# Halves at the sublayer ends, another order in the differential attention, and its causal mask added by TensorE

## The chip, the cores and the metric

One NeuronCore of a Trainium2 chip runs the whole program. The metric is the device time in microseconds; the kernel before takes 2036.5 us (median of 3 runs, 2032.58 to 2038.41).

## The reference

The model has two blocks over 256 tokens of width 1024, in float32. The first block is a four-branch mixer and a mixture of 16 experts. The second has six sublayers, each of the form `x + gate * rmsnorm(f(modulate(rmsnorm(x))))`: feed-forward, sparse attention, feed-forward, then feed-forward, differential attention, feed-forward. The differential attention, cut:

```python
q = apply_rope(proj[..., :B_QK].reshape(B, S, 2, B_HEADS, B_HEAD_DIM), cos, sin)
k = apply_rope(proj[..., B_QK:2 * B_QK].reshape(B, S, 2, B_HEADS, B_HEAD_DIM), cos, sin)
v = proj[..., 2 * B_QK:].reshape(B, S, B_HEADS, B_V_DIM)
s = jnp.einsum('btchd,bschd->bchts', q_b, k32) * scale      # per block of 128 queries
s = jnp.where(causal, s, -jnp.inf)
p = jax.nn.softmax(s, axis=-1)
a = p[:, 0] - lam_val * p[:, 1]
o = jnp.einsum('bhts,bshe->bthe', a, v32)
o = rmsnorm(o, subln_g) * (1.0 - lam_init)
```

## The kernel before

Every engine has its own program, written out by hand; they meet through semaphores. `see(name)` waits for one more count of a name, `mark`, `tell` and a name given to an operation add one. All helpers record one line (`mm` L803, `f` L1740, `stt` L2300, `tt` L2293), so an operation is told by its tiles. Tokens are in two tiles `i` of 128. Weights come in units of 1 MB by SP's queue into a ring of six slots. For products at float32 precision ScalarE rounds a unit (`w_hi`) and VectorE forms the rest (`w_lo`); three matmuls replace one.

**Sublayer ends.** `turnover` (ScalarE and VectorE) and `turn_normed` (TensorE) join two sublayers. For tile 0: when `out` is told, ScalarE takes the squares of the product, VectorE scales it (`out_rows`) and adds it to `xs` (`residual`), ScalarE squares `xs` (`row_squares`), VectorE writes the normed `h` (`pre_norm`, told as `turnable`), and TensorE turns `h` by matmuls with the identity on top of the shift (`turn_normed`, `preset_shift`), from where `columns` takes the operand of the next sublayer. Then tile 1. In a feed-forward, `four_tiles` does four tiles of 128 hidden columns: gate and up of one, down of the one before, for both token tiles; it runs in a loop of four rounds, and two further hidden tiles end the sublayer: down for tile 0, `out`, down for tile 1, `out`.

**Differential attention.** `differential` (TensorE), `a_differential` (ScalarE), `v_differential` (VectorE). Sixteen projection steps give queries and keys (columns 0 to 1023 and 1024 to 2047 of `proj`). VectorE ropes all of them after the last, TensorE turns them in groups of four through banks 2 and 3 and ScalarE copies them to `qT_d` and `kT_d` (`turned`). Eight units `n` follow: query tile `i = n // 4`, two heads of two components each, keys 128 for `i` 0 and 256 for `i` 1. The scores of all units use banks 0 and 1. The order is:

- TensorE, unit n: scores(n+2), values(n+1), a projection step of 24 matmuls whose result later products need, wait for `p_ready`, transposes of the probabilities, wait for ScalarE's copy (`pt_out`), P·V into banks 4 to 7.
- ScalarE, unit n: exponentials of unit n+1 (`softmax_exps`), copy of values(n+1), copy of the transposes, wait for P·V (`o_psum`), and for `i` 1 the square of it.
- VectorE, unit n: `masked_rows` of unit n+1 (scale and mask from PSUM to an SBUF buffer, told as `s_read`; maxima, told as `nmax`), then the reciprocals and the difference of unit n (`p_ready`).

scores(n) wait for `s_read` of unit n-1. Between rope and first unit VectorE also splits unit 11, forms lambda, and prepares the gains and the shift of this and the next sublayer (`out_gain`, `in_gain`, `split_shift`). The sparse sublayer has the same kind of loop, with two bank pairs (`score_bank`), a mask added by a matmul of the identity with `keep`, and exponentials out of PSUM.

Of the kernel before, what the change touches and what calls it, by code (L numbers as in the profile page):

```python
# [21 lines left out]
ALU = mybir.AluOpType  # L22
ACT = mybir.ActivationFunctionType
AX = mybir.AxisListType

S = 256
# [244 lines left out]
def build(nc, A, out):  # L271
# [54 lines left out]
    with ctx:  # L326
# [166 lines left out]
        qT_d, kT_d = by_slot[(first + 6) % R], by_slot[(first + 7) % R]  # L493
# [29 lines left out]
        bigs_d = big_d, acc[:, 0, :].rearrange("p (a b) -> p a b", b=S)  # L523
# [267 lines left out]
        def _(pe):  # L791
# [36 lines left out]
            def turn_normed(n, i):  # L828
# [8 lines left out]
                t.see("turnable")  # L837
                for b in range(2):
                    for k in range(4):
# [492 lines left out]
            def four_tiles(n0, r, h0):  # L1332

                wide = [None, None]
                for f in range(4):
# [10 lines left out]
                    x = down(g, 128, wd, g % 2, r * 4 + (h0 + g + 1), start=False, stop=False)  # L1346
# [164 lines left out]
            def ffn(n):  # L1511
# [6 lines left out]
                with pe.Fori(chunks % 4, 4) as r:  # L1518
                    four_tiles(n0 + 6, r, h0 + 4)
                    if chunks == 4:  # L1520
                        sum_chunk(r, c0)
                m, k0 = n0 + 30, h0 + 20
# [4 lines left out]
                for i in range(2):  # L1527
                    x = down(3, 128, held, 1, k0, False, False, (i,))
# [118 lines left out]
            def differential(sub):  # L1647
                n0 = unit[0]
                for n in range(16):
                    project_step(sub, DIFF_COLS, n)  # L1650
                unit[0] += len(DIFF_COLS)
                values_from = t.sent["proj"]

                def values(n):
# [4 lines left out]
                    t.tell(one_tile(P[:, 3 if n else 7, 0:256], i, w), "proj")  # L1659
# [3 lines left out]
                for i in range(2):  # L1663
                    turns([proj[:, i, 128 * k:128 * k + 128] for k in range(16)])
# [3 lines left out]
                def scores(n):  # L1668
                    i, hg = units[n]
                    kw = 128 * (i + 1)  # L1670
                    if n >= 1:
                        pe.wait_ge(sem("s_read"), n)
                    else:
                        pe.wait_ge(sem("proj_out"), values_from)
                    for k in range(4):
# [4 lines left out]
                               kT_d[r, tile, 0:kw])  # L1680
# [6 lines left out]
                scores(0)  # L1687
                scores(1)
                for n, (i, hg) in enumerate(units):
                    if n + 2 < len(units):  # L1690
                        scores(n + 2)
                    if n + 1 < len(units):
                        values(n + 1)
                    if n == 7:
                        pe.wait_ge(sem("s_read"), 8)
# [40 lines left out]
        def _(act):  # L1736
# [357 lines left out]

            def out_squares(n, i):
# [11 lines left out]
            def turnover(n, kind):  # L2107
# [6 lines left out]
                row_squares(0)  # L2114
# [109 lines left out]
            def values_out(n):  # L2224
# [3 lines left out]
                f(proj[:, i, 2048 + u * 256:2304 + u * 256], P[:, 3 if n else 7, 0:256], ACT.Copy, "proj_out")  # L2228
# [969 lines left out]
```

## Time and profile before

| | us |
|---|---|
| median of 3 runs | 2036.5 |
| profiled execution, device time | 2034.79 |
| its span | 2033.0 |
| busy: TensorE, VectorE, ScalarE, GpSimd | 1913.7, 1396.7, 974.6, 80.4 |
| mean granted TensorE clock | 0.973 |
| code loaded (queue 8) | 1.21 MB, 0.2% of the DMA engines' span |

Times below are microseconds from the first instruction of the span. A bracket behind a row is the engine's idle time before it and who ended that. The granted clock is a share of 2.4 GHz; 0.50 is 1.2 GHz. Matmuls overlap by a few hundredths, so their busy times add to slightly more than the time between starts.

### The profile page before, as it was taken

Reading aid. Unit: us, or ns where it says so; the run is one execution under the profiler, and the core shown is the slowest. Engines: PE = TensorE matmul, PEld = TensorE weight load, DVE = VectorE, ACT = ScalarE, POOL = GpSimd, SP = SyncE. Lnnn points to the kernel's source line nnn. Section 1 sums busy time; section 2 is a strip of 40 time slices with the busy share of each in tenths; the row PEclk is TensorE's granted clock in tenths of the full one; section 3 lists DMA queues with packets and bytes.
Section 4 is the critical chain, followed back from the end, with each engine's and each line's share of the span. In section 5 each row is a group of like instructions: output and inputs, shape, how many; then the busy total and the mean of one; then the engine's idle time right before and its main releaser. Section 6 shows DMA issues by size and latency. Waiting matters only on the chain.

```text
span 2033.0 us, 30145 instructions
## 1 busy us (share of the span) xinstructions
PE 1913.7 (94%) x12007; PEld 1646.7 (81%) x12007; DVE 1396.7 (69%) x1877; ACT 974.6 (48%) x1377; POOL 80.4 (4%) x173
## 2 busy tenths in 40 slices
PE   8999999989899999997999978999999999789998
PEld 7988687878588888876999864899989989648997
DVE  3873444536799889897788684588768875746754
ACT  4664402223577777764333545434444345564432
POOL 6000000000000000000000000000000000000000
PEclk9999999979899999998999989999999999899999
DMA  8443432126999999994897521599579957136652
GB/s 259 148 147 123 145 104 83 43 102 222 390 330 346 349 324 340 367 345 136 302 321 260 192 83 42 202 323 326 175 255 324 324 176 235 44 111 213 215 186 103
DMA packets 214398, 442.84 MB, mean 218 GB/s; under 512 B 8780, under 2 KB 159590, under 8 KB 196880
## 3 DMA queue, kind: packets, MB, share of 16 engines
q1 hardware_dynamic: 207728, 424.70, 60.2%
q0 software_dynamic: 6560, 16.63, 2.4%
q8 instruction: 74, 1.21, 0.2%
q14 instruction: 36, 0.29, 0.0%
HBM read 440.16 MB, written 1.14 MB: 217 GB/s over the span
## 4 chain that ended last, share of the span: by engine, by line
PE 69%; DVE 6%; ACT 5%; issue 1%; DMA 1%; SPq 0%; ACTq 0%; DVEq 0%
PE P L803 68%; ACT merged L1740 1%; DVE w_lo L2347 1%; ACT w_hi L1772 1%; DVE h L2300 1%; ACT sparse_slot L1740 1%; DVE xs L2300 1%; PE P L1415 0%; ACT proj L1740 0%; ACT st L1740 0%; DMA ring<-in_w_down 0%; DMA ring<-in_w_gate 0%; DVE merged L2293 0%; DVE h L3036 0%; DVE st L3034 0%
## 5 line engine op out<-in xcount | busy, mean ns | idle before, releaser
L803 PE MATMUL P<-x_parts,w_hi 128*128 128x256 f32 x2560 | 459.7, 282 | 2.6 <-DVE w_lo L2347 2.6
L803 PEld LDWEIGHTS P<-x_parts,w_hi 128*128 128x128 f32 x2560 | 396.0, 188 | 14.1 <-DVE w_lo L2347 4.6
L2347 DVE TENSOR_TENSOR w_lo<-ring,w_hi 128x1024 fp32r<-128x1024 f32 x302 | 351.9, 1220 | 74.1 <-ACT w_hi L1772 73.9
L803 PE MATMUL P<-w_hi,x_parts 128*128 128x256 f32 (+2 forms) x1504 | 375.5, 336 | 7.3 <-DVE w_lo L2788 4.4
L803 PE MATMUL P<-x_parts,w_lo 128*128 128x256 f32 x1280 | 359.5, 281 | 0.0
L1772 ACT ACTIVATE w_hi<-ring 128x1024 fp32r<-128x1024 f32 x302 | 299.0, 1051 | 85.0 <-DMA ring<-in_ffn_w_down 60.3
L2788 DVE TENSOR_TENSOR w_lo<-ring,w_hi 128x1024 fp32r<-128x1024 f32 x240 | 280.7, 1221 | 29.9 <-ACT w_hi L2010 27.3
L803 PEld LDWEIGHTS P<-w_hi,x_parts 128*128 128x128 f32 x1504 | 259.5, 192 | 42.8 <-issue 11.0
L2010 ACT ACTIVATE w_hi<-ring 128x1024 fp32r<-128x1024 f32 x240 | 240.9, 1052 | 87.5 <-DMA ring<-in_w_up 32.6
L803 PEld LDWEIGHTS P<-x_parts,w_lo 128*128 128x128 f32 x1280 | 241.1, 188 | 0.0
L803 PE MATMUL P<-w_lo,x_parts 128*128 128x256 f32 (+2 forms) x752 | 235.3, 334 | 0.0
L803 PE MATMUL P<-w_hi,hid_hi 128*128 128x512 f32 x512 | 202.5, 396 | 1.4 <-DVE hid_lo L2293 1.4
L803 PE MATMUL P<-w_hi,hid_lo 128*128 128x512 f32 x512 | 202.4, 395 | 0.0
L803 PE MATMUL P<-w_lo,hid_hi 128*128 128x512 f32 x512 | 202.3, 395 | 0.0
L1996 ACT ACTIVATE silu<-P 128x256 f32<-128x256 f32 x88 | 33.8, 384 | 323.9 <-PE P L803 300.6
L803 PEld LDWEIGHTS P<-w_lo,x_parts 128*128 128x128 f32 x752 | 145.5, 194 | 13.5
L2758 DVE TENSOR_TENSOR hid<-silu,P 128x256 f32<-128x256 f32 (+1 forms) x80 | 33.6, 420 | 120.9 <-ACT silu L1996 120.7
L803 PEld LDWEIGHTS P<-w_hi,hid_lo 128*128 128x128 f32 x512 | 95.9, 187 | 23.5
L803 PEld LDWEIGHTS P<-w_hi,hid_hi 128*128 128x128 f32 x512 | 96.2, 188 | 21.5 <-DVE hid_lo L2293 1.6
L803 PEld LDWEIGHTS P<-w_lo,hid_hi 128*128 128x128 f32 x512 | 96.0, 188 | 19.8
L803 PE MATMUL P<-xT,ring 128*128 128x256 f32 x448 | 106.7, 388 | 2.7 <-DMA ring<-in_w_in 2.1
L803 PE MATMUL P<-xm_hi,w_lo 128*128 128x256 f32 x352 | 100.9, 287 | 0.0
(507 smaller groups left out, 2718.6 us busy)
## 6 DMA issues: line engine op xcount, KB each, us to landing
mod_w<-in_ada_w SPq DMA_DIRECT2D x52, 1024.0 KB, 10.1
ring<-in_ffn_w_gate SPq DMA_DIRECT2D x44, 1024.0 KB, 5.5
ring<-in_ffn_w_up SPq DMA_DIRECT2D x44, 1024.0 KB, 10.0
ring<-in_ffn_w_down SPq DMA_DIRECT2D x44, 1024.0 KB, 5.0
ring<-in_w_in SPq DMA_DIRECT2D x40, 1024.0 KB, 5.7
ring<-in_w_gate SPq DMA_DIRECT2D x40, 1024.0 KB, 4.9
ring<-in_w_up SPq DMA_DIRECT2D x40, 1024.0 KB, 5.0
ring<-in_w_down SPq DMA_DIRECT2D x40, 1024.0 KB, 5.2
```

The lines of the kernel that those rows point to most:

```text
L803: return pe.matmul(o, l, r, start=start, stop=stop, **kw)
L1740: a.done(act.activation(o, i, fn, **kw), name)
L1772: act.activation(w_hi[:, slot, c:c + half], ring[:, slot, c:c + half], ACT.Copy).then_inc(sem("w_hi"), 1)
L1996: act.activation(silu[:, k % 2, :], P[:, k % 2, 0:S], ACT.Silu).then_inc(sem("silu"), 1)
L2010: act.activation(w_hi[:, n % R, c:c + UNIT // 2], ring[:, n % R, c:c + UNIT // 2], ACT.Copy).then_inc(sem("w_hi"), 1)
L2300: v.done(dve.scalar_tensor_tensor(out=o, in0=x, scalar=s, in1=y, op0=op0, op1=op1), name)
L2347: dve.tensor_tensor(w_lo[:, slot, c:c + half], ring[:, slot, c:c + half], w_hi[:, slot, c:c + half].bitcast(F32), ALU.subtract).then_inc(s ...
L2758: dve.tensor_tensor(x, silu[done:128, k % 2, :], P[done:128, k % 2, S:2 * S], ALU.mult).then_inc(sem("hid_part"), 1)
L2788: dve.tensor_tensor(w_lo[:, n % R, c:c + UNIT // 2], ring[:, n % R, c:c + UNIT // 2], w_hi[:, n % R, c:c + UNIT // 2].bitcast(F32), ALU.su ...
```

## The change

1. `turn_normed` waits for `turnable` twice for tile 0, once per half of the columns; `pre_norm` writes `h` of tile 0 in two halves. `residual` does so for `xs` of tile 0, and ScalarE squares these halves one by one (`row_squares_halves`).
2. In the last round of a feed-forward the down product of hidden tile 2 is done for token tile 0 alone; for tile 1 it comes behind the first `out`. TensorE's loop has three rounds and the fourth is written out.
3. Differential attention: VectorE ropes the queries in the middle of the projection, then half of the keys, and the other half behind lambda, gains and mask. TensorE turns the queries behind steps 12 and 13, the keys of tile 0 before scores(0), those of tile 1 behind it, then values(1), then scores(1); in the loop values(n+2) stand in place of values(n+1). `qT_d` lies in `rowbc`.
4. The mask is rounded to `keep` and added in the score banks by two matmuls a unit. `masked_rows` is gone; maxima and exponentials read PSUM, and scores(n) wait for the exponentials of unit n-1.

```diff
@@ turn_normed
-                t.see("turnable")
                 for b in range(2):
+                    if b == 0 or i == 0:
+                        t.see("turnable")
@@ four_tiles(n0, r, h0, last_down=(0, 1))
+                    x = down(g, 128, wd, g % 2, r * 4 + (h0 + g + 1), start=False, stop=False, tiles=last_down if f == 3 else (0, 1))
@@ ffn
-                with pe.Fori(chunks % 4, 4) as r:
+                with pe.Fori(chunks % 4, 3) as r:
...
+                four_tiles(n0 + 6, 3, h0 + 4, (0,))
...
                 for i in range(2):
+                    if i:
+                        down(2, 128, held, 0, k0 - 1, False, False, (i,))
                     x = down(3, 128, held, 1, k0, False, False, (i,))
@@ differential (TensorE)
                 for n in range(16):
                     project_step(sub, DIFF_COLS, n)
+                    if n == 12:
+                        t.see("roped")
+                    if n in (12, 13):
+                        turn_heads(n - 12, 0)
...
                 values(0)
                 t.see("roped")
-                for i in range(2):
-                    turns([proj[:, i, 128 * k:128 * k + 128] for k in range(16)])
+                turn_heads(0, D)
                 pe.wait_ge(sem("turned"), t.sent["turn"])
...
                     if n >= 1:
-                        pe.wait_ge(sem("s_read"), n)
+                        pe.wait_ge(sem("exps"), 8 + n)
...
+                    for b in range(2):
+                        mm(P[:, b, :].rearrange("p (c s) -> p c s", s=S)[:, :, 0:kw], ident_r,
+                           keep[:, 0, S - kw:S].unsqueeze(1).to_broadcast([128, 2, kw]), stop=False, skip_group_check=True)
...
                 scores(0)
+                t.see("roped")
+                turn_heads(1, D)
+                values(1)
                 scores(1)
+                pe.wait_ge(sem("turned"), t.sent["turn"])
                 for n, (i, hg) in enumerate(units):
                     if n + 2 < len(units):
                         scores(n + 2)
-                    if n + 1 < len(units):
-                        values(n + 1)
+                    if n + 2 < len(units):
+                        values(n + 2)
@@ row_squares_halves (ScalarE), new
+                one, two = st[:, 12 + i:13 + i], st[:, 14 + i:15 + i]
+                a.see("row")
+                f(acc[:, i, 0:512], xs[:, i, 0:512], ACT.Square, accum_out=one)
+                f(one, one, ACT.Identity, scale=1 / D, bias=eps_ln[:, 1:2])
+                a.see("row")
+                f(acc[:, i, 512:D], xs[:, i, 512:D], ACT.Square, accum_out=two)
+                f(st[:, 8 + i:9 + i], two, ACT.Sqrt, "row_rs", scale=1 / D, bias=one)
@@ a_differential
+                a_project(n, {12: lambda: head_columns(0, qT_d), 13: lambda: head_columns(1, qT_d)})
                 values_out(0)
                 high(unit[0], (11,))
...
-                softmax_exps(0, 0, bigs_d)
+                softmax_exps(0, 0, bigs_d, halves(0), 64 ** -0.5)
+                values_out(1)
                 for n in range(8):
                     i, hg = n // 4, n % 4
                     if n < 7:
-                        softmax_exps(n + 1, (n + 1) // 4, bigs_d)
-                        values_out(n + 1)
+                        softmax_exps(n + 1, (n + 1) // 4, bigs_d, halves(0), 64 ** -0.5)
+                        if n < 6:
+                            values_out(n + 2)
@@ pre_norm (VectorE)
-                stt(h[:, i, :], xs[:, i, :], st[:, 8 + i:9 + i], pre_scale, ALU.mult, ALU.mult, "turnable")
+                for c in (slice(0, D),) if i else (slice(0, 512), slice(512, D)):
+                    stt(h[:, i, c], xs[:, i, c], st[:, 8 + i:9 + i], pre_scale[:, c], ALU.mult, ALU.mult, "turnable")
@@ residual
+                for c in (slice(0, 512), slice(512, D)) if i == 0 and n < 5 else (slice(0, D),):
+                    stt(xs[:, i, c], h[:, i, c], st[:, 16 + i:17 + i], xs[:, i, c], ALU.mult, ALU.add,
+                        "x_final" if n == 5 else "row")
@@ score_peaks
-                v.done(dve.tensor_reduce(st[:, c:c + 4], halves(score_bank(n))[:, :, 0:kw], AX.X, ALU.max))
+                v.done(dve.tensor_reduce(st[:, c:c + 4], halves(bank)[:, :, 0:kw], AX.X, ALU.max))
@@ v_differential
-                low(unit[0], range(2, 10))
-                dve.wait_ge(sem("proj_out"), proj_before[0] + 16)
+                low(unit[0], range(2, 8))
+                dve.wait_ge(sem("proj_out"), proj_before[0] + 8)
                 for i in range(2):
-                    apply_rope(i, 0, 32)
+                    apply_rope(i, 0, 16)
                 v.mark("roped")
+                low(unit[0], (8, 9))
+                dve.wait_ge(sem("proj_out"), proj_before[0] + 12)
+                for i in range(2):
+                    apply_rope(i, D, 8)
                 low(unit[0], (10, 11))
...
                 copy(hid[:, 0, 128:256], causal_neg[:, :])
+                copy(ident_r, ident[:, :])
+                copy(keep[:, 0, :], hid[:, 0, :], "kept")
+                for i in range(2):
+                    dve.wait_ge(sem("proj_out"), proj_before[0] + 15 + i)
+                    apply_rope(i, D + 512, 8)
+                    v.mark("roped")
...
-                masked_rows(0, 0, mask[0], bigs_d)
+                score_peaks(0, 0, 0)
```

## Rows read from the trace of the kernel before

**Rows 1.** The page's busy times, shares of the span and instructions.

```profile
PE 1913.7 (94%) x12007; PEld 1646.7 (81%) x12007; DVE 1396.7 (69%) x1877; ACT 974.6 (48%) x1377; POOL 80.4 (4%) x173
```

**Rows 2.** Windows: busy us (instructions) by engine, granted clock, DMA share, GB/s.

```profile
1727.55:1745.54 17.99, 8.98 (x58) 7.42 (x57) 14.03 (x27) 9.04 (x14) 0.00 (x0) 0.81 0.18 59
...
1755.71:1791.16 35.45, 30.38 (x239) 26.90 (x240) 23.68 (x51) 20.03 (x62) 0.00 (x0) 1.00 0.30 92
```

**Rows 3.** Timeline of TensorE in unit 5: start, us, engine, line, tiles, shapes.

```profile
1779.05 1.14 PE L803 MATMUL P<-w_hi_slot 64*128 64x256 f32 x8
...
1784.43 1.16 PE L803 MATMUL P<-proj 128*128 128x128 f32 x8 [0.81 <-ACT proj L1740]
```

**Rows 4.** Windows: values cold, warm; two sublayer starts; sparse loop; three half tiles.

```profile
1749.43:1754.05 4.62, 4.62 (x28) 4.60 (x26) 3.62 (x13) 2.69 (x12) 0.00 (x0) 0.63 0.00 0
...
1756.29:1759.39 3.10, 3.10 (x28) 3.08 (x26) 2.53 (x7) 1.48 (x6) 0.00 (x0) 1.00 0.01 3
...
1141.04:1148.91 7.87, 7.87 (x51) 7.87 (x51) 3.31 (x5) 1.83 (x4) 0.00 (x0) 0.72 0.93 324
...
1678.90:1684.77 5.87, 5.87 (x50) 5.71 (x49) 3.96 (x6) 1.97 (x5) 0.51 (x1) 1.00 1.09 365
...
1203.00:1220.00 17.00, 11.69 (x47) 6.74 (x47) 14.52 (x41) 8.76 (x31) 0.00 (x0) 0.51 0.00 1
...
1669.30:1673.54 4.24, 4.24 (x20) 3.14 (x18) 2.83 (x4) 2.33 (x7) 0.00 (x0) 1.00 0.33 102
```

**Rows 5.** Timeline of ScalarE behind a P·V.

```profile
1785.68 0.60 ACT L1740 ACTIVATE h<-P 128x512 f32<-128x512 f32 x1 [1.31 <-PE P L803]
```

**Rows 6.** Timeline of TensorE: turns of tile 0 at four sublayer ends.

```profile
1137.34 2.62 PE L803 MATMUL P<-ident,h 128*128 128x128 f32 x16 [2.13 <-DVE h L2300]
...
1275.21 2.05 PE L803 MATMUL P<-ident,h 128*128 128x128 f32 x16 [1.18 <-DVE h L2300]
...
1476.26 3.53 PE L803 MATMUL P<-ident,h 128*128 128x128 f32 x16 [2.13 <-DVE h L2300]
...
1676.30 2.05 PE L803 MATMUL P<-ident,h 128*128 128x128 f32 x16 [2.13 <-DVE h L2300]
```

**Rows 7.** Timeline of ScalarE: exponentials from PSUM, sparse sublayer.

```profile
1209.80 0.37 ACT L1740 ACTIVATE sparse_slot<-P,st 128x128 f32<-128x128 f32 x1
...
1222.87 0.47 ACT L1740 ACTIVATE sparse_slot<-P,st 128x256 f32<-128x256 f32 x1
...
1225.03 0.19 ACT L1740 ACTIVATION_READ_ACCUMULATOR sparse_slot<-P,st 128x1 f32 x1
```

**Rows 8.** Timeline of TensorE: mask matmuls, scores and a late product, sparse sublayer.

```profile
1195.26 0.50 PE L803 MATMUL P<-hid_lo,hid_hi 128*128 128x256 f32 x2 [0.61 <-ACT sparse_slot L1740]
...
1195.69 0.71 PE L803 MATMUL P<-sparse_slot 64*128 64x128 f32 x8
...
1231.77 0.73 PE L803 MATMUL P<-hid_lo,hid_hi 128*128 128x512 f32 x2
...
1232.43 1.13 PE L803 MATMUL P<-sparse_slot 64*128 64x256 f32 x8
...
1241.34 1.98 PE L803 MATMUL P<-sparse_slot,proj 128*64 128x256 f32 x8 [3.18 <-ACT sparse_slot L1740]
```

**Rows 9.** Timeline of VectorE and TensorE ahead of the first scores.

```profile
1733.66 1.09 PE L1545 MATMUL P<-ident,proj 128*128 128x128 f32 x8 [2.47 <-DVEq L268]
...
1733.71 4.63 DVE L2347 TENSOR_TENSOR w_lo<-ring,w_hi 128x1024 fp32r<-128x1024 f32 x4 [0.16 <-ACT w_hi L1772]
...
1739.78 3.50 PE L1545 MATMUL P<-ident,proj 128*128 128x128 f32 x16 [5.03 <-ACT w_hi_slot L1740]
...
1742.93 0.23 DVE L2303 COPY hid<-causal_neg 128x128 f32<-128x128 f32 x1
```

**Rows 10.** Timeline of VectorE: a weight split in the differential projection, of three alike.

```profile
1712.45 2.36 DVE L2347 TENSOR_TENSOR w_lo<-ring,w_hi 128x1024 fp32r<-128x1024 f32 x2 [3.24 <-ACT w_hi L1772]
```

**Rows 11.** Timeline of VectorE: `h` of tile 0.

```profile
1674.95 1.28 DVE L2300 SCALAR_TENSOR_TENSOR h<-xs,st,xT 128x1024 f32<-128x1024 f32 x1
```

More of the change, by code:

```diff
@@ L492, in build @@
         by_slot = [buf("w_hi_slot%d" % k, 128, DT, S, ctx=m2) for k in range(R)]
-        qT_d, kT_d = by_slot[(first + 6) % R], by_slot[(first + 7) % R]
+        qT_d, kT_d = rowbc[:, 2:4, :].rearrange("p a (b s) -> p (a b) s", s=S), by_slot[(first + 7) % R]
         m2.close()
@@ L1521, in ffn @@
                         sum_chunk(r, c0)
+                four_tiles(n0 + 6, 3, h0 + 4, (0,))
+                if chunks == 4:
+                    sum_chunk(3, c0)
                 m, k0 = n0 + 30, h0 + 20
@@ L1679, in scores @@
                         x = mm(P[:, k // 2, (k % 2) * S:(k % 2) * S + kw], qT_d[r, tile, i * 128:i * 128 + 128],
-                               kT_d[r, tile, 0:kw])
+                               kT_d[r, tile, 0:kw], start=False, skip_group_check=True)
                     t.tell(x, "s_psum")
@@ L1691, in differential @@
                         scores(n + 2)
-                    if n + 1 < len(units):
-                        values(n + 1)
+                    if n + 2 < len(units):
+                        values(n + 2)
                     if n == 7:
-                        pe.wait_ge(sem("s_read"), 8)
+                        pe.wait_ge(sem("exps"), 16)
                         pe.wait_ge(sem("proj_out"), values_from + 8)
@@ L2113, in turnover @@
                     return
-                row_squares(0)
+                row_squares_halves(0)
                 if kind == "ffn":
@@ L2923, in residual @@
                 recip(st[:, 16 + i:17 + i], st[:, 16 + i:17 + i])
-                stt(xs[:, i, :], h[:, i, :], st[:, 16 + i:17 + i], xs[:, i, :], ALU.mult, ALU.add,
-                    "x_final" if n == 5 else "row")
+                for c in (slice(0, 512), slice(512, D)) if i == 0 and n < 5 else (slice(0, D),):
+                    stt(xs[:, i, c], h[:, i, c], st[:, 16 + i:17 + i], xs[:, i, c], ALU.mult, ALU.add,
+                        "x_final" if n == 5 else "row")
             def turnover(n, kind):
@@ L3002, in apply_rope, with score_peaks @@
                 tt(x2, w[2], w[3], ALU.add)
-            def score_peaks(n, i):
+            def score_peaks(n, i, bank):
                 kw, c = 128 * (i + 1), 24 + 8 * (n % 2)
                 v.see("s_psum")
-                v.done(dve.tensor_reduce(st[:, c:c + 4], halves(score_bank(n))[:, :, 0:kw], AX.X, ALU.max))
+                v.done(dve.tensor_reduce(st[:, c:c + 4], halves(bank)[:, :, 0:kw], AX.X, ALU.max))
                 ts(st[:, c:c + 4], st[:, c:c + 4], -64 ** -0.5, name="nmax")
-            def masked_rows(n, i, mask, pair):
-                kw, big, c = 128 * (i + 1), pair[n % 2], 24 + 8 * (n % 2)
-                v.see("s_psum")
-                s4 = halves(0)[:, :, 0:kw]
-                stt(big[:, :, 0:kw], s4, 64 ** -0.5, over(mask, 4), ALU.mult, ALU.add, "s_read")
-                v.done(dve.tensor_reduce(st[:, c:c + 4], big[:, :, 0:kw], AX.X, ALU.max))
-                ts(st[:, c:c + 4], st[:, c:c + 4], -1.0, name="nmax")
             def row_parts(n, pair):
@@ L3140, in v_differential @@
                     if n < 7:
-                        masked_rows(n + 1, (n + 1) // 4, mask[(n + 1) // 4], bigs_d)
+                        score_peaks(n + 1, (n + 1) // 4, 0)
                     big_n, c = row_parts(n, bigs_d)
```

25 lines of the change are left out of this document (14 added, 11 removed).

## The prediction, on record before the result

> **What bounds the kernel now.** I began at the page's busy times. TensorE is busy for 94% of the span, VectorE for 69% and ScalarE for 48% [rows 1], so time is mostly lost wherever TensorE stands still or runs at the lower of its two clocks (granted 0.50, against 1.00). Then I cut the differential sublayer, the main place of the change, into stretches by windows [rows 2]. From the end of its projection (1727.55) to its first scores (1745.54) TensorE works half the time. From the end of the first P·V product (1755.71) to that of the seventh (1791.16) it works 30.38 of 35.45 us at the full clock. The timeline inside the second stretch [rows 3] says what a unit is to TensorE: scores 1.14 us, 24 value matmuls 3.1 [rows 4], transposes 0.6, a hole of 0.81 in which ScalarE copies the transposes, P·V 1.16. The next scores begin where P·V ends, without a hole. So the loop is bound by TensorE in order of issue, and any wait put ahead of the scores is paid in full. ScalarE squares the output of the unit before, 0.60 us [rows 5], and goes straight on to its four exponentials, which run beside the next unit's matmuls.
>
> At the ends of sublayers TensorE waits for VectorE's `h`: 2.13 us behind each of three feed-forward sublayers, 1.18 behind an attention [rows 6].
>
> **The loop: what replaces what.** Scores live in one bank pair (0 and 1). Before, VectorE emptied it with the masked product (`s_read`) and TensorE never waited for that, because values, transposes and P·V of a unit stood in between. Now scores(n+2) wait for the exponentials of unit n+1 (`exps`). ScalarE issues these behind its wait for P·V(n-1), which is the last thing TensorE did before it reached scores(n+2). The two are thus in series: P·V ends, 0.1 us of signal, exponentials, 0.05 us, scores. Behind the blocked scores TensorE holds values, transposes and P·V, and for those ScalarE and VectorE wait in turn, so nothing fills it.
>
> Price: four exponentials out of PSUM take 2.35 us (1222.87 to 1225.22) at 256 keys, and at 128 keys, where one is 0.37 us and not 0.47, four tenths less, 1.93 [rows 7]. These rows are of the same helper in the sparse sublayer, where it reads PSUM already. In the second half the square of 0.60 us stands ahead of them [rows 5]. The mask's two matmuls add 0.43 us at 128 keys and 0.66 us at 256, start to start [rows 8]. Removing VectorE's masked product (0.69 us, later 1.22) gives nothing inside the loop, since its maxima are ready long before ScalarE starts.
>
> Unit by unit, from the end of one P·V to the next, new against old (5.35, 5.73, 5.85, 6.48, 6.47, 5.57, from the timeline's ends):
> - to P·V(1): 2.1 wait + 1.1 scores and mask + 3.1 values + 0.4 + 0.75 + 0.7 = 7.9 (some ends overlap), +2.6.
> - P·V(2): the scores are now of 256 keys, 1.8: 8.7, +3.0. P·V(3): exponentials of 256 keys: 9.1, +3.2.
> - P·V(4): transposes 0.6 and P·V 1.16: 9.7, +3.2. P·V(5): the square comes in as well, 10.4, +3.9.
> - P·V(6): no values left to do; square, exponentials, copy of the transposes, product: 4.8, -0.8.
>
> Sum +15.1 us. The last unit and the head sums stay as they are.
>
> **Ahead of the loop.** Sixteen transposes of the queries go into the projection, TensorE-bound there, so they cost their 2 x 1.09 us [rows 9] and only move. The rope of the queries and of half the keys goes into VectorE's idle time between weight splits, 3.24 us before each [rows 10], and costs nothing; without that cover it would be some 6 us. But the rope of the other keys now stands behind VectorE's split of unit 11, lambda and the two gains. In the old trace that run goes from 1733.71 to 1743.16, which held nobody up much, TensorE being late anyway [rows 9]. New, in the old trace's clock: projection ends 1729.8, values(0) 1733.4, ScalarE splits unit 11, VectorE's half is done 1737.4, lambda, gains and copies (4.8 us, as before) and two copies for the mask (0.5) 1742.7, first key rope 1744.1 (six operations of some 0.23 us, the time of the row of the 128-element copy), eight transposes and two copies of 0.6, scores(0) at 1746.7 (before: 1745.54). They end at 1748.2. Now eight more transposes and values(1) stand ahead of scores(1), and ScalarE has two more copies ahead of exps(0), which end about 1752.0; scores(1) end 1753.6; maxima 1.0; exps(1) to 1756.6, for which scores(2) wait; scores(2), values(2), transposes, copy, P·V(0) to 1762.4. Before it was 1755.71: +6.7 us, of which 3.1 is the work of values(2), taken back in the loop above. Bounds for this part: +3 if the keys' rope costs half, +9 if TensorE is at the low clock throughout.
>
> A rule of the Trainium skill speaks against this loop (Perfetto Trace Analysis, section Matmuls): independent matmul groups should rotate through different PSUM banks, so that ScalarE's or VectorE's emptying of one runs beside the matmuls of the next. The sparse sublayer does so with two bank pairs, and there the mask and scores of its steady part follow without a wait [rows 8]; the differential loop got by with one pair because its reader was quick. By that rule the price is the whole emptying, which is what the sum above takes.
>
> **The clock.** Holes of this size bring it down. After 2.13 us of idleness it fell in two of three sublayer ends (transposes of 2.62 and 3.53 us, against 2.05 [rows 6]); after 3.18 us it fell in the sparse loop (the product behind it takes 1.98 us, 1.09 at the full clock [rows 8]). Holes of 0.81 us did not do so. A fall costs 1.5 us where it meets one block of values (4.62 against 3.10 us) and 2.0 us at a sublayer's start (7.87 against 5.87) [rows 4]. The new loop has seven holes of 2.1 to 3.2 us. I take five falls of 1.6 us: +8. Bounds: nothing, if the values between keep it up; about +20, if it stays down as in the sparse sublayer's first half (mean 0.51 over 17 us [rows 4]).
>
> **The sublayer ends.** One half tile of the down product (1.4 us: 4.24 us for three [rows 4]) moves behind the first `out`, so VectorE's chain starts 1.4 us sooner against the same TensorE work. `h` of the first tile comes in halves of about 0.7 us (1.28 whole [rows 11]), so the first four transposes can start 0.6 us sooner and the last eight matmuls follow 1.42 us behind the chain's end, instead of sixteen behind 1.28. The residual in halves gives nothing: square 0.6, read 0.1, an added scaling of 0.3, square, root come to the same 2.8 us as one square of 1.06 behind a 1.28 us product. After the transposes VectorE's second-tile chain binds, which is 1.3 us earlier. So: +1.3 us at the third feed-forward end, 1.5 at the second, 3.9 at the first, whose low clock (2.6 us of it) I count as gone; 0.6 at each of three others. Sum -8.5 us; bounds -3 (clock lost all the same, half the chain eaten) and -11. The last `out` is not moved, and the tail neither. One of the four rounds of TensorE's loop unrolled: one branch less and more code to load, against the 1.21 MB that the page shows for the whole span, and no hole of TensorE put down to it in these windows; between -0.5 and +1, taken as nothing. SP's queue and POOL's get no instruction, and weight slots are freed at the same points.
>
> **Sum.** 15.1 + 6.7 + 8 - 8.5 = +21 us on the profiled 2034.8 (span 2033.0), thus 2056. That execution lies 1.7 us under the median of the runs, so 2057.
>
> **Rivals.**
> - The clock holds through the loop: +13.3, about 2049. For it: full clock in the old loop and in most of the sparse loop with 1.45 us holes. Against: the falls at 2.13 us. Chance 0.22.
> - The clock stays down: +20 instead of +8, 2069. For it: the 17 us at 0.51. Against: these had only 11.7 us of work in 17; the new loop has more. 0.18.
> - The new wait is covered, the other side: the exponentials would end before TensorE reaches the scores, as if issued ahead of the P·V wait. The waits of 2.1 to 3.2 us (12.3 in the loop, 3 ahead of it) and the falls go: 21 - 15.3 - 8 = -2, 2034, and from there the ends decide: if they give their 11 instead of 8.5, and the code nothing, 2030. It decides from the point where values take longer than ScalarE's square and exponentials together, and these are issued first. Against: ScalarE's program order. 0.12 for this, halved between no change and faster.
> - The change's first aim fails the other way: `h` in halves and the moved tile give nothing, since the second tile's chain is the late one: 2063. 0.06.
>
> The forecast itself has 0.42. What differs by less than 0.3% (6 us) I call no change. Range 2040 to 2070: it takes the first two rivals and their bounds, and leaves the covered wait outside. Slower 0.88, same 0.06, faster 0.06.
>
> **What would show it.** In the new profile TensorE's scores (or the mask's matmuls) should show holes of 2 to 3 us, released by the exponentials, once a unit; units of 8 to 10 us; the granted clock at 0.50 in several of them; scores(0) no earlier than before against the projection's start; at the feed-forward ends a hole well under 1 us. If the holes ahead of the mask's matmuls are missing, the forecast is wrong at its main step; if they are there with a clock of 1.00, the first rival is right.

## The result, and the profile after

The changed kernel takes 2060.1 us (median of 4 runs, 2056.1 to 2064.6) beside 2037.5 for the kernel before on the same chip: ratio 1.0113, 95% interval 1.0090 to 1.0136, 22.7 us between the medians. Forecast: 2057, 2040 to 2070. Its profiled execution took 2059.7 us, with a span of 2058.0 and a mean granted clock of 0.970.

The page of after, busy times and loaded code (answer to [rows 1]):

```profile
PE 1924.1 (93%) x12023; PEld 1651.7 (80%) x12023; DVE 1394.6 (68%) x1906; ACT 975.5 (47%) x1392; POOL 82.0 (4%) x173
...
q8 instruction: 81, 1.33, 0.3%
```

Busy times hardly say anything; the answer is in one sublayer. The windows below cut both kernels at the same points, the ends of the turns of the second token tile in each sublayer, so each row runs from one sublayer's start to the next's (feed-forward, sparse, feed-forward, feed-forward, differential). First the kernel before:

```profile
949.20:1150.69 201.49, 198.71 (x1392) 181.88 (x1392) 155.10 (x185) 83.97 (x116) 8.53 (x15) 0.98 0.77 266
1150.69:1288.12 137.43, 112.56 (x673) 80.65 (x672) 86.01 (x187) 67.73 (x154) 3.15 (x6) 0.93 0.30 100
1288.12:1488.16 200.04, 197.18 (x1393) 180.69 (x1392) 153.06 (x184) 83.17 (x115) 8.46 (x15) 0.99 0.77 268
1488.16:1686.78 198.62, 195.76 (x1392) 179.23 (x1392) 154.87 (x185) 83.97 (x116) 8.44 (x15) 1.00 0.78 270
1686.78:1842.99 156.21, 133.24 (x852) 105.95 (x852) 87.38 (x145) 85.90 (x171) 2.63 (x5) 0.95 0.37 119
```

and the kernel after:

```profile
950.50:1148.10 197.60, 195.90 (x1393) 179.24 (x1392) 155.26 (x187) 84.45 (x119) 8.56 (x15) 1.00 0.78 270
1148.10:1284.68 136.58, 112.27 (x673) 80.35 (x672) 86.42 (x189) 68.32 (x157) 3.15 (x6) 0.93 0.32 103
1284.68:1482.48 197.80, 195.86 (x1392) 179.24 (x1392) 153.38 (x186) 83.79 (x118) 8.51 (x15) 1.00 0.78 271
1482.48:1680.06 197.58, 195.83 (x1392) 179.22 (x1392) 155.16 (x187) 84.61 (x119) 8.42 (x15) 1.00 0.79 270
1680.06:1867.86 187.80, 147.01 (x868) 116.54 (x868) 84.44 (x165) 85.21 (x174) 2.62 (x5) 0.88 0.31 100
```

The first four are 8.0 us shorter together (3.9, 0.9, 2.2, 1.0); the differential sublayer is 31.6 us longer, at a granted clock of 0.88 instead of 0.95. With 1.3 us more ahead of 949.20 and 0.1 behind, that is the 25.0 us between the spans.

Inside the differential sublayer, windows of after (answer to [rows 2]): from the end of the projection to the mask of the first scores, and from the end of P·V(0) to that of P·V(6).

```profile
1722.85:1740.14 17.29, 5.04 (x32) 4.44 (x33) 9.87 (x27) 5.45 (x8) 0.00 (x0) 0.70 0.18 61
1759.49:1818.17 58.68, 39.08 (x226) 31.54 (x226) 18.14 (x46) 18.77 (x61) 0.00 (x0) 0.83 0.23 72
```

35.45 us of loop became 58.68. TensorE's timeline of after shows where; its rows with a hole in front of 1 us or more, from the head to P·V(6):

```profile
1737.42 1.97 PE L1551 MATMUL P<-ident,proj 128*128 128x128 f32 x8 [10.97 <-DVEq L268]
...
1752.16 0.47 PE L803 MATMUL P<-hid_lo,hid_hi 128*128 128x256 f32 x2 [3.19 <-ACT proj L1761]
...
1761.56 0.50 PE L803 MATMUL P<-hid_lo,hid_hi 128*128 128x256 f32 x2 [2.07 <-ACT merged L1761]
...
1769.46 0.73 PE L803 MATMUL P<-hid_lo,hid_hi 128*128 128x512 f32 x2 [2.07 <-ACT proj L1761]
...
1780.08 0.72 PE L803 MATMUL P<-hid_lo,hid_hi 128*128 128x512 f32 x2 [2.50 <-ACT merged L1761]
...
1790.75 0.98 PE L803 MATMUL P<-hid_lo,hid_hi 128*128 128x512 f32 x2 [2.50 <-ACT proj L1761]
...
1802.65 1.22 PE L803 MATMUL P<-hid_lo,hid_hi 128*128 128x512 f32 x2 [3.14 <-ACT merged L1761]
...
1816.10 2.07 PE L803 MATMUL P<-proj 128*128 128x128 f32 x8 [3.33 <-ACT proj L1761]
```

`P<-hid_lo,hid_hi` are the mask's two matmuls, the first thing of a unit's scores. Each waits for ScalarE, for the tile (`merged` or `proj`) that the last exponential wrote. The last row is P·V(6), which has no scores ahead of it any more and waits for ScalarE's copy. ScalarE's timeline of after, behind P·V(4):

```profile
1799.61 0.60 ACT L1761 ACTIVATE h<-P 128x512 f32<-128x512 f32 x1 [1.31 <-PE P L803]
1800.24 0.47 ACT L1761 ACTIVATE merged<-P,st 128x256 f32<-128x256 f32 x1
...
1802.03 0.47 ACT L1761 ACTIVATE merged<-P,st 128x256 f32<-128x256 f32 x1
```

P·V(4) ends at 1799.51, the square starts 0.10 later, four exponentials follow, and TensorE goes on at 1802.65: the series of the forecast.

### The profile page after: what moved, and what is told of

Its sections match the earlier page's. It is cut to its first block, busy times and chain, and to the rows that moved or that the text cites. A ratio compares the mean times of both kernels' runs of the same rounds, so it can differ in the third digit from the quotient of the medians.

```text
span 2058.0 us, 30194 instructions
## 1 busy us (share of the span) xinstructions
PE 1924.1 (93%) x12023; PEld 1651.7 (80%) x12023; DVE 1394.6 (68%) x1906; ACT 975.5 (47%) x1392; POOL 82.0 (4%) x173
## 3 DMA queue, kind: packets, MB, share of 16 engines
q8 instruction: 81, 1.33, 0.3%
## 4 chain that ended last, share of the span: by engine, by line
PE 66%; DVE 8%; ACT 6%; DMA 1%; issue 1%; SPq 0%; ACTq 0%; DVEq 0%
PE P L803 65%; ACT merged L1761 2%; DVE w_lo L2383 1%; DVE h L2336 1%; ACT proj L1761 1%; DMA ring<-in_w_gate 1%; ACT w_hi L1793 1%; DVE xs L2336 1%; ACT sparse_slot L1761 1%; DVE w_lo L2824 1%; DMA ring<-in_w_branch 1%; ACT st L1761 0%; PE P L1416 0%; DVE merged L2329 0%; PE P L1551 0%
## 5 line engine op out<-in xcount | busy, mean ns | idle before, releaser
L803 PEld LDWEIGHTS P<-xT,ring 128*128 128x128 f32 x448 | 86.3, 198 | 18.0 <-issue 4.2
```

The lines of the kernel that those rows point to most:

```text
L803: return pe.matmul(o, l, r, start=start, stop=stop, **kw)
```

## Experiments

Every kernel was timed beside the kernel before on its chip; where a ratio is turned into microseconds, before is taken at 2036. "Diff." is the differential sublayer between the cuts used above, "loop" the time from the end of P·V(0) to that of P·V(6), "four" the four sublayers ahead, all from the one profiled execution, so a single sample each.

| kernel | ratio to before, 95% | diff. | loop | four |
|---|---|---|---|---|
| before | | 156.2 | 35.45 | 737.6 |
| after | 1.0113 (1.0090 to 1.0136) | 187.8 | 58.68 | 729.6 |
| parts 1 and 2 | 0.9933 (0.9913 to 0.9954) | 155.9 | 35.39 | 733.5 |
| parts 3 and 4 | 1.0162 (1.0131 to 1.0192) | 187.8 | 58.58 | 737.7 |
| part 3 alone | 0.9999 (0.9978 to 1.0020) | 157.8 | 35.12 | 736.4 |
| part 4 alone | 1.0121 (1.0094 to 1.0148) | 187.9 | 61.00 | 737.6 |
| after, exponentials early | 1.0017 (1.0001 to 1.0034) | 169.6 | 38.40 | 729.7 |
| after, holes filled | 1.0057 (1.0036 to 1.0078) | 179.7 | 50.74 | 730.4 |
| other head | 0.9921 (0.9901 to 0.9940) | 146.9 | 35.91 | 729.7 |
| transposes first | 0.9901 (0.9878 to 0.9925) | 143.9 | 32.06 | 729.3 |
| part 1 alone | 1.0021 (1.0009 to 1.0033) | 158.1 | 35.46 | 737.6 |
| part 2 alone | 0.9970 (0.9955 to 0.9984) | 157.3 | 35.43 | 729.4 |
| late gains | 0.9896 (0.9874 to 0.9918) | 143.0 | 28.70 | 729.7 |
| late gains, no part 1 | 0.9897 (0.9882 to 0.9912) | 141.7 | 28.73 | 729.2 |

**The parts by themselves.** Each is the kernel before with the named parts of the diff above, no other edit.

> The kernel before with parts 1 and 2 of the change alone (halves at the sublayer ends, the down tile of hidden tile 2 moved behind the first out). Theory: the two parts of the change add up and this one gives -8.5 us by the prediction's terms, about -10 by the marks in the trace of after, so 0.995 to 0.996 of the kernel before, about 2028; TensorE's idle time ahead of the turns of tile 0 falls from 2.13 us to under 0.8 at the feed-forward ends. Rival (the ends give nothing, because the second token tile's chain is the late one): within 2 us of before.

> The kernel before with parts 3 and 4 alone (the differential sublayer). Theory: +29 us by the prediction's terms (15.1 loop, 6.7 ahead of it, 8 clock), +32 by the trace of after, so 2066 to 2069, ratio about 1.015; the holes of 2.1 to 3.3 us ahead of the mask's matmuls stand as in after. Rival (part of the loss comes from the sublayer ends, their buffers or the unrolled code, or the two parts meet): clearly less, under +25.

The loss is wholly in parts 3 and 4: their sublayer takes 187.8 us, as in after. The ends give 0.67%, 13.6 us; that is more than the 8.0 us that the traces of after show in the four sublayers. This kernel's own profiled execution shows only 4.1, because its sparse sublayer ran at 140.6 us against 136.6 in after, with the same code. The clock did that: both have a hole of 3.18 us ahead of the same product, and the 13 us from that product on, first in this kernel and then in after, have a granted clock (seventh value) of 0.50 and 0.88:

```profile
1237.12:1250.12 13.00, 11.70 (x31) 5.66 (x32) 4.87 (x5) 5.86 (x8) 0.00 (x0) 0.50 0.00 0
```

```profile
1238.49:1251.49 13.00, 11.56 (x40) 5.82 (x41) 4.86 (x5) 5.86 (x8) 0.00 (x0) 0.88 0.00 0
```

Then the differential sublayer was split. Part 3 alone keeps VectorE's masked product and the wait for `s_read`, and leaves out the mask matmuls. Against the changed kernel, cut:

```diff
+                stt(big[:, :, 0:kw], s4, 64 ** -0.5, over(mask, 4), ALU.mult, ALU.add, "s_read")
...
-                        pe.wait_ge(sem("exps"), 8 + n)
+                        pe.wait_ge(sem("s_read"), n)
...
-                softmax_exps(0, 0, bigs_d, halves(0), 64 ** -0.5)
+                softmax_exps(0, 0, bigs_d)
```

> The kernel before with part 3 alone: the new order of ropes, turns and values in the differential sublayer, but the masked product into SBUF and the wait for it (s_read) are kept, with no mask matmuls. Theory (the loss of the loop is the wait for the exponentials): no hole over 1 us ahead of scores(2) to scores(7), the granted clock stays at 1.00 behind P.V(0), loop from P.V(0) to P.V(6) about 3 us shorter than before since values(1) are done ahead of it; what is left is the head, where the late ropes and eight turns cost 4 to 10 us: in all between +1 and +7 us. Rival A (the order itself is what costs): +15 or more. Rival B (order is a gain once the wait is gone): below -2.

> The kernel before with part 4 alone: order of before, but mask by matmuls, maxima and exponentials from PSUM, scores waiting for the exponentials. Theory: the same holes of 2.1 to 3.2 us ahead of the mask's matmuls in every unit and falls of the clock; periods of the units as in after, and one wait less ahead of the loop: +18 to +27 us, most of the differential's +29 to +32. Rival (the wait only hurts in the new order, because values(n+2) and not values(n+1) stand behind the scores): under +10.

Part 4 alone has the whole loss of the sublayer (187.9 us), with the holes of 2.07 to 3.13 us at the same matmuls; part 3 alone has 1.6 us of the 31.6. By the times the agreement is looser: part 4 costs 24.6 us and the two parts together 33.0, with intervals that overlap. Three rows of TensorE's timeline of part 3 alone, and then the window of its loop:

```profile
1748.73 1.97 PE L1545 MATMUL P<-ident,proj 128*128 128x128 f32 x8 [10.38 <-DVEq L268]
...
1759.33 0.72 PE L803 MATMUL P<-w_hi_slot,rowbc 64*128 64x128 f32 x8 [0.96 <-DVE proj L2316]
...
1798.61 1.22 PE L803 MATMUL P<-proj 128*128 128x128 f32 x8 [3.47 <-ACT proj L1751]
```

```profile
1764.71:1799.83 35.12, 27.67 (x216) 24.18 (x216) 24.00 (x54) 19.64 (x61) 0.00 (x0) 1.00 0.37 121
```

The wait for `s_read` shows once (0.96 us ahead of scores(2)), then never. But the order gives nothing in the loop either: values(1) were taken out of it (3.1 us), and where values(7) used to stand, ahead of P·V(6), TensorE now waits 3.47 us for ScalarE, which does the exponentials of unit 7 before it copies the transposes of unit 6. I had expected 3 us less there.

**The wait itself.** ScalarE gets its exponentials one unit earlier; all else is after.

```diff
                 values_out(1)
+                softmax_exps(1, 0, bigs_d, halves(0), 64 ** -0.5)
...
-                    if n < 7:
-                        softmax_exps(n + 1, (n + 1) // 4, bigs_d, halves(0), 64 ** -0.5)
-                        if n < 6:
-                            values_out(n + 2)
-                    else:
+                    if n < 6:
+                        softmax_exps(n + 2, (n + 2) // 4, bigs_d, halves(0), 64 ** -0.5)
+                        values_out(n + 2)
+                    elif n == 7:
```

> The changed kernel with one thing moved: ScalarE issues the exponentials of every unit one unit earlier, exps(1) behind values_out(1) and exps(n+2) in unit n, so that they no longer stand behind its wait for P.V(n) when TensorE reaches scores(n+3). Mask matmuls, maxima and exponentials from PSUM and the order of values stay. Theory (the loss is the series P.V, exponentials, scores): the holes of 2.1 to 3.2 us ahead of the mask's matmuls fall to under 1 us, the granted clock stays at 1.00 behind P.V(0), and about 15 us of waits and 8 us of clock come back of the changed kernel's 2060: near 2037, at most 2043. Rival (the bank pair itself is too few, since scores, maxima and exponentials of one unit fill the pair for about 5 us whoever issues them first, and the wait only moves to another place): under 8 us back, 2052 or more.

Window of the loop and two rows of TensorE's timeline in it:

```profile
1760.33:1798.73 38.40, 29.68 (x225) 25.09 (x225) 18.13 (x46) 16.92 (x53) 0.00 (x0) 1.00 0.34 109
```

```profile
1779.69 0.71 PE L803 MATMUL P<-proj 128*128 128x128 f32 x4 [1.77 <-ACT proj L1761]
1780.16 0.71 PE L803 MATMUL P<-hid_lo,hid_hi 128*128 128x512 f32 x2
```

The hole ahead of the mask is gone and the clock is 1.00: 20.3 of the 23.2 us that the loop had lost come back, with the same mask matmuls, the same bank pair and the same operations on every engine. In four units about 1 us moved ahead of P·V, where ScalarE's copy of the transposes now stands behind the exponentials (1.77 instead of 0.81). The ratio, 1.0017, answers 2039, at the upper side of what was expected.

So the order of the reader decided. The rule weighed in the prediction (the Trainium skill, Perfetto Trace Analysis, section Matmuls: rotate groups through PSUM banks) is kept by neither kernel; by it the pair should still have cost its emptying here, and no hole ahead of these scores inside the loop shows one. No run gave the differential loop a second bank pair, so what that would bring is not shown.

**The clock.** Products that nobody reads fill the holes of after, a little short of each:

```diff
                 for n, (i, hg) in enumerate(units):
+                    for k in range((22, 14, 14, 18, 18, 23, 23, 0)[n]):
+                        mm(P[:, 2, 0:256], x_hi[:, k % 8, 0:128], x_hi[:, (k + 1) % 8, :])
```

> The changed kernel with products that nobody reads (fp32r, 128x128 on 128x256, 14 to 23 of them, 0.117 us each) put into the holes ahead of the scores of the loop, a little fewer than fill each hole; they change nothing in the output. Theory (the short waits lower TensorE's clock and that costs a second time): the granted clock stays at 1.00 in the loop, P.V(0) to P.V(6) takes 51 instead of 58.7 us, the kernel about 8 us less than the changed one: 2052. Rival A (the falls cost nothing, since the waits behind them shrink by as much): no difference within 3 us. Rival B (the products delay the scores): longer by 1 us or more a unit.

```profile
1759.41:1810.15 50.74, 44.12 (x335) 38.51 (x335) 17.77 (x46) 18.76 (x61) 0.00 (x0) 1.00 0.26 84
```

```profile
1784.75 2.39 PE L803 MATMUL P<-x_parts 128*128 128x256 f32 x18
1787.49 0.73 PE L803 MATMUL P<-hid_lo,hid_hi 128*128 128x512 f32 x2 [0.35 <-ACT proj L1763]
```

The mask's matmuls still wait for ScalarE (0.35 us behind the fillers here, 0.35 to 0.41 in all units), so nothing was delayed and no wait was removed; the loop is 7.94 us shorter through the clock alone. Over the sublayer it is 8.1 us: 1.9 more came ahead of the loop and 1.7 were lost again behind it. By the ratios it is about 11. This also makes the units comparable with the forecast, which had counted the clock apart. From P·V end to P·V end:

| unit to P·V | 1 | 2 | 3 | 4 | 5 | 6 |
|---|---|---|---|---|---|---|
| forecast | 7.9 | 8.7 | 9.1 | 9.7 | 10.4 | 4.8 |
| holes filled, clock 1.00 | 7.89 | 8.62 | 9.08 | 9.71 | 10.34 | 5.10 |
| after | 7.90 | 10.18 | 10.69 | 11.25 | 12.82 | 5.84 |

**What was late ahead of the loop.** Parts 1 to 3, without part 4; VectorE's and TensorE's work behind the projection in another order:

```diff
@@ VectorE
-                low(unit[0], (10, 11))
...
+                low(unit[0], (10,))
                 for i in range(2):
                     dve.wait_ge(sem("proj_out"), proj_before[0] + 15 + i)
                     apply_rope(i, D + 512, 8)
                     v.mark("roped")
...
                 masked_rows(0, 0, mask[0], bigs_d)
+                low(unit[0], (11,))
@@ TensorE
                 values(0)
                 t.see("roped")
                 turn_heads(0, D)
+                t.see("roped")
+                turn_heads(1, D)
...
                 scores(0)
-                t.see("roped")
-                turn_heads(1, D)
                 values(1)
                 scores(1)
```

Lambda's products and the mask go ahead of `low(10)`; ScalarE rounds unit 11 behind its copies of the keys; `out_gain`, `in_gain` and `split_shift` go into units 0, 1 and 2.

> Parts 1, 2 and 3 of the change without part 4, and another order ahead of the loop: VectorE forms lambda during the projection, splits unit 10 before and unit 11 behind the rope of the last keys, and prepares the gains and the next shift inside units 0 to 2; both tiles of keys are turned behind values(0); ScalarE splits unit 11 behind the copies of the keys. Theory (what the new order lost ahead of the loop is VectorE's row of work between projection and last rope, the hole of 10 to 11 us): the hole falls below 3 us, P.V(0) ends 7 to 12 us earlier against the start of the sublayer than with part 3 alone; with the 13.6 us that the sublayer ends gave, 2036 - 13.6 - 7 to 12 = 2011 to 2016. Rival (that work only moves into the loop and is late there, units of 1.5 us more): near 2022, as the ends alone.

TensorE's timeline, first and second key tile:

```profile
1726.12 1.03 PE L1551 MATMUL P<-ident,proj 128*128 128x128 f32 x8
...
1729.00 1.19 PE L1551 MATMUL P<-ident,proj 128*128 128x128 f32 x8 [1.84 <-ACT w_hi_slot L1757]
```

The hole of 10 us is 1.84; P·V(0) ends 61.2 us after the sublayer's cut instead of 72.5 with part 3 alone and 68.9 before. At 0.9921 (2020 against a before of 2036) the kernel is 4 us above what I expected, though the sublayer gained what it should: the 13.6 us of the ends did not add in full. The 16.1 us of the ratio fit the trace, 7.9 of the four sublayers and 9.3 of this one.

**Transposes ahead of values.** In units 1 to 5 of TensorE's program, with ScalarE's copies in the same order:

```diff
-                    if n + 2 < len(units):
+                    if n + 2 < len(units) and n == 0:
                         values(n + 2)
...
                     t.tell(x, "pt")
+                    if 0 < n < 6:
+                        values(n + 2)
                     pe.wait_ge(sem("pt_out"), t.sent["pt"])
```

> As the kernel with the other head order, and in units 1 to 5 TensorE does the transposes of the probabilities before values(n+2), and ScalarE copies them before the copy of values(n+2), so that the values cover the copy for which P.V(n) waits. Theory: the hole of 0.73 to 0.81 us ahead of P.V goes in five units, 4 us less than with the other head order alone. Rival (the probabilities are not ready that early, or ScalarE is late with the copy because four exponentials stand ahead of it): no gain, or up to 3 us more.

The holes ahead of P·V are gone in units 1 to 5 and the loop is 3.9 us shorter; new ones stand ahead of the transposes, put down to VectorE (1.56 us in unit 1), and 2.31 us ahead of P·V(6). The next kernel aims at these: `out_gain` and `in_gain` behind unit 7, `split_shift` behind the normed outputs, and ScalarE's copy of unit 6 before the exponentials of unit 7.

> As the kernel with the transposes of the probabilities ahead of the values, and: VectorE prepares the output gain and the next input gain behind the last unit and splits the next shift behind the four normed outputs, instead of in units 0 to 2; ScalarE copies the transposes of unit 6 before the exponentials of unit 7. Theory: the holes of 1.56, 0.43 and 0.25 us ahead of the transposes of units 1, 3 and 4, put down to VectorE, go, and that of 2.31 us ahead of P.V(6) falls to 0.8; 3 to 4 us less, about 2009. Rival (VectorE's normed outputs at the end wait for the gains, or the last unit for its exponentials): the end of the sublayer gives it back, no difference.

```profile
1743.50:1772.20 28.70, 26.36 (x216) 23.67 (x216) 22.42 (x48) 18.39 (x57) 0.00 (x0) 1.00 0.43 138
```

TensorE is now busy for 26.36 of 28.70 us, and the loop is 3.4 us shorter, but the sublayer only 0.9: 2.5 us come back behind P·V(6), as the rival had it: 0.5 up to P·V(7), 2.0 behind it. Which of its two waits takes them was not followed. The ratio, 0.9896, cannot be told from 0.9901.

**The ends, part by part.** The kernel before with one part of the two, no other edit.

> Part 1 of the change alone: residual, squares and h of tile 0 in halves, and TensorE's turns of tile 0 waiting for each half; the down product is not moved. Theory (the first four turns start 0.6 us sooner at each of six ends, and the end of the last ones does not move): 0.1 us at each of six ends, the hole ahead of the turns about 1.5 us behind a feed-forward and 0.7 behind an attention, in all 2 to 5 us less than before, the larger end where the shorter hole keeps the clock up. Rival (most of what both parts give, 11 to 13 us by the times, is of this part): 8 us less or more.

> Part 2 of the change alone: in the last round of each feed-forward the down product of hidden tile 2 for token tile 1 stands behind the first out (five feed-forward ends before a next sublayer or the last one), TensorE's fourth round written out; nothing in halves. Theory: VectorE's chain for tile 0 starts 1.4 us sooner at each of three ends, the hole ahead of the turns goes from 2.13 to about 0.75 us, and the clock no longer falls at the two ends where it did: 5 to 8 us less than before. With part 1 alone it adds up to what both gave (0.9933 of before). Rival (only both together get under the length at which the clock falls): 2 us or less for each alone.

By the times the two together give 13.6 us, the tile alone 6, the halves alone minus 4. By the traces the tile alone gives 8.2 us in the four sublayers and both together 8.0 (in after), the halves alone nothing. TensorE's turns of tile 0, first the halves alone at the three feed-forward ends, then the tile alone at the same three; sixteen turns take 2.05 us at the full clock:

```profile
1132.33 3.55 PE L803 MATMUL P<-ident,h 128*128 128x128 f32 x16 [1.72 <-DVE h L2311]
...
1469.18 2.57 PE L803 MATMUL P<-ident,h 128*128 128x128 f32 x16 [1.91 <-DVE h L2311]
...
1670.24 2.05 PE L803 MATMUL P<-ident,h 128*128 128x128 f32 x16 [1.72 <-DVE h L2311]
```

```profile
1132.05 2.05 PE L803 MATMUL P<-ident,h 128*128 128x128 f32 x16 [0.74 <-DVE h L2305]
...
1466.80 2.05 PE L803 MATMUL P<-ident,h 128*128 128x128 f32 x16 [0.73 <-DVE h L2305]
...
1663.96 2.05 PE L803 MATMUL P<-ident,h 128*128 128x128 f32 x16 [0.73 <-DVE h L2305]
```

What differed was open, so the last kernel takes part 1 out of the best one:

> The kernel with the late gains, without part 1 of the change: the moved down tile stays, residual, squares and h of tile 0 are whole again. What is open: in the traces the four sublayers ahead of the differential one are 8.0 us shorter with both parts and 8.2 us shorter with the moved tile alone, so the halves give nothing; in the times both parts gave 0.9933 of before and the tile alone 0.9970. Theory (the traces are right): the ratio to before is that of the kernel with the late gains, 0.9896, within 0.002. Rival (the halves are worth what the times of both parts say, 0.0037 of the whole): 0.9925 or more.

0.9897 against 0.9896: the halves give nothing that the times can see, and the rival's 0.0037 is outside what the intervals leave; a difference of about 5 us either way is not. The windows of the four sublayers without the halves say what is behind the zero:

```profile
949.13:1146.34 197.21, 195.79 (x1392) 179.23 (x1392) 154.79 (x185) 83.97 (x116) 8.57 (x15) 1.00 0.78 269
1146.34:1283.96 137.62, 112.87 (x673) 80.75 (x672) 86.00 (x187) 67.72 (x154) 3.15 (x6) 0.91 0.31 104
1283.96:1481.16 197.20, 195.74 (x1392) 179.27 (x1392) 153.14 (x184) 83.36 (x115) 8.46 (x15) 1.00 0.78 271
1481.16:1678.35 197.19, 195.73 (x1392) 179.22 (x1392) 154.72 (x185) 83.85 (x116) 8.44 (x15) 1.00 0.78 271
```

With the halves (late gains) the same four took 197.59, 136.73, 197.77 and 197.60: they cost 0.4 to 0.6 us at each feed-forward end and give 0.9 at the end of the sparse sublayer, where no tile was moved. Why both parts alone on the kernel before timed at 0.9933, and not at 0.9970, stays open.

## Why the prediction was right, point by point

- **Loop, +15.1.** Right: at the full clock the loop takes 50.74 us, 15.3 more than before, and each unit but the last is within 0.1 us of its forecast. The last had 0.3 too little.
- **The wait is the cause, by ScalarE's program order.** Shown: with the exponentials issued earlier 20.3 of 23.2 us return, and part 4 alone has all the loss. My rival of the covered wait stood at 2034; with its condition met in the loop it came to about 2039. The loop is not the reason: it had 15.1 less 12.3, +2.8 us, and took +2.9. That is partly luck, since units 2 to 5 are some 0.6 us longer each than the rival leaves them, ScalarE's copy being late in place of the scores, and the last unit is 2.3 shorter. The head is the reason: P·V(0) ends 10.4 us later against the cut than before, where the rival had 3.7. The hole of 3.19 us ahead of scores(2), which I had let go, stayed, and the head's clock was lost there too.
- **The clock, +8.** In the loop 7.9, from falls in the five units behind the first, 1.6 us each: the number and the price that I had taken. The number was a choice between none and seven, so that it met is luck in part. Windows of after for the periods to P·V(1), P·V(2) and P·V(5), granted clock 1.00, 0.83 and 0.73:

```profile
1759.49:1767.39 7.90, 5.09 (x41) 4.41 (x40) 2.55 (x8) 2.60 (x10) 0.00 (x0) 1.00 0.00 0
1767.39:1777.57 10.18, 7.30 (x40) 5.78 (x40) 3.08 (x8) 2.60 (x10) 0.00 (x0) 0.83 0.05 5
...
1799.51:1812.33 12.82, 8.87 (x49) 7.18 (x49) 3.48 (x8) 3.84 (x11) 0.00 (x0) 0.73 0.28 84
```

  The step that was too small is the clock ahead of the loop: P·V(0) ended 36.6 us behind the projection, not 32.6. Ropes and first turns were on time (14.6 us behind it, forecast 14.3), and so were scores(0) (17.3, forecast 16.9). But TensorE was at the low clock behind its hole of 10.97 us: turns of 1.97 instead of 1.09, values(1) 4.4 instead of 3.1, so that scores(2) came 2.5 us late, and values(2) fell to it again. My upper bound for the head, +9, was exceeded: 2.0 for the longer projection and 8.5 behind it are +10.5.
- **Behind the loop** 2.1 us came back where I had -0.6; no run isolates why. Sum for the sublayer: 2.0 + 8.5 + 23.2 - 2.1 = +31.6, forecast +29.2.
- **The ends, -8.5.** -8.0 in four sublayers, where the forecast had 7.3 of its 8.5 (3.9 first, 1.5 second, 1.3 third, 0.6 behind the sparse one; measured 3.9, 2.2, 1.0, 0.9). I had credited the halves with 0.6 us at each of three ends. At the sparse one they gave it (0.9). At the feed-forward ends, where the sum took them as harmless, they cost 0.4 to 0.6 us: what they gain ahead of the turns (at the third end a hole of 0.33 instead of 0.73 us) they lose behind them, in a hole of 0.50 that the tile alone does not have, and in one of 0.20 ahead of the second tile's turns; I had followed VectorE's chain only as far as `h`, not to the copies `x_parts` behind it. TensorE's timeline of after, third feed-forward end (answer to [rows 6]):

```profile
1668.79 2.05 PE L803 MATMUL P<-ident,h 128*128 128x128 f32 x16 [0.33 <-DVE h L2336]
1670.77 0.70 PE L803 MATMUL P<-pick,shift_parts 40*128 40x512 f32 x2
...
1671.97 0.36 PE L803 MATMUL P<-w_hi,x_parts 128*128 128x256 f32 x1 [0.50 <-DVE x_parts L2339]
```

- **The unrolled round** loads 0.12 MB more code (1.33 against 1.21; the tile alone has it, the halves alone do not), and no wait is put down to it: nothing, as taken.

- **Rivals.** The last two were added up wrongly: ends that give nothing make 2057 + 8.5, nearly 2066 and not 2063, and ends of 11 us take the covered wait from 2034 to about 2031.5, not 2030. Neither changes the forecast.

On the spans the sum missed by 3.7 us, +25.0 for +21.3. The head alone missed by 3.8. Behind the loop and at the four ends 2.2 more came back than forecast, and outside the five sublayers 2.0 more were lost (1.4 longer, where 0.6 shorter was forecast); these nearly cancel. So 2057 for 2060 flatters the sum a little; the units do not.

## What to carry to other kernels

Before a reader of a PSUM bank is made slower, or moved from one engine to another, look at what stands ahead of it in that engine's program, and not only at how long it takes: here the same four exponentials a unit cost 20 us more in one place of ScalarE's list than one unit earlier. Price a short repeated wait twice, once as the wait and once as the clock that falls behind it; filling the wait with useless matmuls measures the second by itself. And follow a chain that is cut in halves to the last operation that somebody waits for.

## What the runs showed of the hardware

- The clock fell behind holes of 1.72 and 1.91 us, and behind another of 1.72 it did not. The windows of part 1 alone over the turns behind its three feed-forward holes give the granted clock (seventh value) 0.54, 0.77 and 1.00:

```profile
1132.33:1135.88 3.55, 3.55 (x17) 3.33 (x17) 3.29 (x5) 1.03 (x4) 0.74 (x2) 0.54 1.10 349
1469.18:1471.74 2.56, 2.56 (x17) 2.33 (x17) 2.33 (x4) 1.03 (x4) 0.00 (x0) 0.77 1.09 359
...
1670.24:1672.30 2.06, 2.06 (x17) 1.94 (x17) 1.99 (x3) 0.56 (x3) 0.00 (x0) 1.00 1.10 348
```

  Yet with the exponentials early, holes of 1.74 to 1.77 us in four units running left it at 1.00 over the whole loop, and behind the first hole of 2.07 us of after it was 1.00 up to P·V(1). How long it stays down differs as well: behind the same hole of 3.18 us the next 13 us had 0.50 in one execution and 0.88 in another (above). The length of a hole alone does not tell.
- Stretches mostly repeat to some tenths between kernels (differential sublayer 187.8, 187.8 and 187.9 us; feed-forward 197.6), while whole executions of one kernel differ by 10 us. Much of that lies ahead of the first cut, where the kernels hardly differ: that stretch took 944.0 to 955.7 us in the profiled executions, at a granted clock of 0.98 in the shortest and 0.96 in the longest. A stretch with holes can do it too: the sparse sublayer took 136.4 to 137.6 us in thirteen kernels and 140.6 in one, and the differential sublayer, with the loop of before, 155.9 to 158.1. For a local change the cut stretch is the sharper measure if its clock is read with it, and the times are the check on it.
